# Six SBUF homes instead of seven for the experts' gate/up weights, with the residual x left in place

## The reference

```python
x = x + mixer(rmsnorm(x, norm_mix[i]))
h = rmsnorm(x, norm_ffn[i])
# router: best group of 4, then the best 2 of its 8 experts, with their gates -> combine
hid = silu(einsum('td,edf->tef', h, w_gate)) * einsum('td,edf->tef', h, w_up)
x = x + einsum('tef,efd->td', hid * combine[..., None], w_down)
```

## Time and profile before

| | |
|---|---|
| median of 3 runs | 1291.3 us (1290.79 to 1293.12) |
| the profiled execution, own time | 1287.51 us |
| its span | 1285.7 us |
| PE busy | 1138.3 us (89%) |
| DVE, ACT, POOL busy | 530.9, 379.7, 388.3 us |
| DMA | 278.21 MB, mean 216 GB/s |
| chain that ended last | PE 63%, DMA 14%, DVE 10%, SP's queue 7%, ACT 4% |

### The profile page before, as it was taken

One profiled execution on the slowest core, in us unless ns is written; L12 is line 12 of the kernel. 1 busy time (PEld: TensorE's weight loads), 2 busy tenths in 40 slices (PEclk: granted clock), 3 DMA queues, 4 the chain that ended last, 5 costly groups with the idle time before them and its releaser, 6 DMA issues.

```text
span 1285.7 us, 21203 instructions
## 1 busy us (share of the span) xinstructions
PE 1138.3 (89%) x8573; PEld 796.6 (62%) x8573; DVE 530.9 (41%) x1202; ACT 379.7 (30%) x838; POOL 388.3 (30%) x428
## 2 busy tenths in 40 slices
PE   5999999799999883989779999779999899999792
PEld 4866678555555442868568887568888555555341
DVE  4466763411111115565685455764653411111114
ACT  3426841111111012364453445443522011111010
POOL 1334521122322211057545366442301022322210
PEclk9999999899999896989899999899999799999997
DMA  7121047999999998011000130001458899999996
GB/s 239 66 73 67 2 197 282 379 375 384 380 383 381 384 396 316 11 66 66 1 3 2 66 117 15 2 3 65 165 182 328 345 365 383 386 384 379 379 392 248
DMA packets 67793, 278.21 MB, mean 216 GB/s; under 512 B 16888, under 2 KB 16984, under 8 KB 43120
## 3 DMA queue, kind: packets, MB, share of 16 engines
q1 hardware_dynamic: 56480, 255.89, 52.4%
q0 software_dynamic: 11072, 20.43, 4.7%
q10 hardware_dynamic: 144, 0.52, 0.1%
HBM read 265.83 MB, written 27.26 MB: 228 GB/s over the span
## 4 chain that ended last, share of the span: by engine, by line
PE 63%; DMA 14%; DVE 10%; SPq 7%; ACT 4%; issue 2%; POOL 1%; DVEq 0%; POOLq 0%
PE bank L1101 11%; PE bank L150 9%; PE bank L152 9%; PE bank L151 9%; DMA hn<-in_moe_w_up 5%; PE bank L1110 5%; SPq L2332 4%; PE bank L1643 4%; PE bank L1093 3%; DMA ring<-in_moe_w_up 3%; DMA arena<-in_moe_w_up 2%; SPq L2338 2%; DMA ring<-in_gdn_w_in 2%; PE bank L519 2%; PE bank L528 1%
## 5 line engine op out<-in xcount | busy, mean ns | idle before, releaser
L978 POOL DMA_INDIRECT y_rows<-arena,idx_i x64 | 64.6, 1010 | 348.5 <-DVE arena L1287 343.5
L1192 ACT ACTIVATE arena<-bank 128x128 f32<-128x128 f32 x64 | 17.8, 277 | 367.2 <-PE bank L1101 202.0
L1291 DVE TENSOR_TENSOR arena<-arena,bank 128x128 f32<-128x128 f32 x64 | 18.4, 288 | 258.3 <-ACT arena L1192 258.3
L152 PE MATMUL bank<-ring_r,ht_r 128*128 128x512 f32 x288 | 113.1, 393 | 0.0
L1101 PE MATMUL bank<-ring,arena 128*64 128x256 f32 x832 | 101.6, 395 | 8.9 <-DMA ring<-in_moe_w_up 7.9
L1287 DVE COPY arena<-bank 128x512 f32<-128x512 f32 x64 | 44.3, 692 | 143.9 <-PE bank L1110 143.9
L150 PE MATMUL bank<-ring_r,arena_r 128*128 128x512 f32 (+1 forms) x228 | 91.5, 401 | 4.8 <-DVE ring_r L174 4.8
L151 PE MATMUL bank<-ring_r,arena_r 128*128 128x512 f32 x224 | 88.0, 393 | 0.0
L1101 PEld LDWEIGHTS bank<-ring,arena 128*64 128x64 f32 x832 | 57.6, 136 | 44.1 <-DMA ring<-in_moe_w_up 8.9
L151 PE MATMUL bank<-ht_r,ring_r 128*128 128x512 f32 (+1 forms) x224 | 81.8, 365 | 0.0
L1093 PEld LDWEIGHTS bank<-ident,arena 64*128 64x128 f32 x512 | 61.3, 201 | 28.4 <-issue 25.1
(11 more groups left out here) (339 smaller groups left out, 2342.9 us busy)
## 6 DMA issues: line engine op xcount, KB each, us to landing
ring<-in_moe_w_gate SPq DMA_DIRECT2D x26, 1024.0 KB
ring<-in_moe_w_up SPq DMA_DIRECT2D x26, 1024.0 KB
arena<-in_moe_w_down SPq DMA_DIRECT2D x24, 1024.0 KB
ring<-in_moe_w_down SPq DMA_DIRECT2D x24, 1024.0 KB
ring<-in_gdn_w_in SPq DMA_DIRECT2D x8, 2048.0 KB, 8.3
arena<-in_moe_w_gate SPq DMA_DIRECT2D x10, 1024.0 KB
arena<-in_moe_w_up SPq DMA_DIRECT2D x10, 1024.0 KB
ht<-in_moe_w_gate SPq DMA_DIRECT2D x10, 1024.0 KB
```

The source lines that it names most:

```text
L152: return pe.matmul(dst, a[1], b[0], start=False, stop=stop)
L978: pool.indirect_dma_start(out=y_rows[l], out_offset=bass.IndirectOffsetOnAxis(ap=idx_i[:, 1, e:e + 1], axis=0), in_=y_out[:, e % RING, :], ...
```

## The change

Home 6 is gone, with the store of x, the read-back, and the waits on both. Expert e uses gate/up home e mod 6 up to e = 30, and expert 31 uses home 3. The homes of the down matrices and the waits on all other homes are as before. The order of SP's queue is otherwise unchanged.

```diff
-        x_rows = [dram(f"x_rows{l}", [SEQ, D]) for l in range(2)]
...
-        GU_SLOTS, DN_SLOTS = 7, 8
+        GU_SLOTS, DN_SLOTS = 6, 8
...
-                   ht[:, :, :].rearrange("p c n -> p (c n)"), hn[:, :, :].rearrange("p t n -> p (t n)"),
-                   x[:, :, :].rearrange("p t n -> p (t n)")]
-        X_HOME, GAIN2_HOME = 6, 7
+                   ht[:, :, :].rearrange("p c n -> p (c n)"), hn[:, :, :].rearrange("p t n -> p (t n)")]
+        GAIN2_HOME = 7
...
-        GU_OF = [e % GU_SLOTS for e in range(EXPERTS - 4)] + [0, 3, 4, 5]
+        GU_OF = [e % GU_SLOTS for e in range(EXPERTS - 1)] + [3]
...
-        x_kept, x_again = sem("x_kept"), sem("x_again")
...
         def combine_best(dve, t, o):
-            if t == 0:
-                dve.wait_ge(x_again, 16 * TT)
...
         def finish_dve(dve, o):
-            dve.wait_ge(x_again, 16 * TT * 2)
...
-            x_spilled = [(x_kept, 16 * TT * (l + 1)), (ln["rows"], TT * (2 * l + 2))]
-            gu_freed = [None, half_way, half_way, done, [(s["routed"], TT * (l + 1))], kept_rows, x_spilled]
+            gu_freed = [None, half_way, half_way, done, [(s["routed"], TT * (l + 1))], kept_rows]
...
-            for t in range(TT):
-                sp.wait_ge(x_half, 2 * TT * l + TT + t + 1)
-                sp.dma_start(x_rows[l][t * P:(t + 1) * P, :], x[:, t, :]).then_inc(x_kept, 16)
             load_gate_up(sp, l, 3, gu_freed[3])
             for k in (4, 5, 6):
                 load_down(sp, l, k, dn_freed[k])
-            for e in (4, X_HOME, 5):
+            for e in (4, 5):
                 load_gate_up(sp, l, e, gu_freed[e])
             for e in range(GU_SLOTS, EXPERTS):
                 load_gate_up(sp, l, e, None)
...
-            sp.wait_ge(s["up"], EXPERTS * l + max(e for e in range(EXPERTS) if GU_OF[e] == X_HOME) + 1)
-            for t in range(TT):
-                sp.dma_start(x[:, t, :], x_rows[l][t * P:(t + 1) * P, :]).then_inc(x_again, 16)
```

## The result

The changed kernel takes 1297.87 us in the median of ten runs, against 1291.43 for the kernel before: ratio 1.0053, 95% interval 1.0038 to 1.0069, so 5 to 9 us slower. The forecast was 1300.6 us (9.3 us slower) with a range of 1295 to 1308. The profiled execution of the changed kernel took 1295.35 us, its span is 1293.4 us, 7.7 us more than before.

The account below looks back on a forecast made before the run. The prediction took the arrival of the last gate/up pair to bound each expert loop. Plus 3.1 us at layer 0's combine and 6.2 us in layer 1's loop made 9.3 us, from 1291.3 to 1300.6 us, range 1295 to 1308.

Parts of the forecast that it names:

- What bounds: Both expert loops: the arrival of the last gate/up pair, expert 31's, sets the end, at 482.3 and 1254.6 us.
- Store: Ahead of each loop: dropping the 2 MiB store of x is worth 0, at best 0 to 1 us.
- One pair moves: Start of each loop: 77 MiB instead of 75 pass between hn's pair and expert 31's, 5.4 us more (4.9 to 6.2).
- Expert 31 waits for gate/up of 27: End of each loop: expert 31's home frees later, but over 20 us of transfers are still queued, so 0.
- One down matrix slips: Start of each loop: down 8 queues behind pair 8, the second step issues 2 MiB instead of 3, costing 0.8 us.
- Read-back in layer 1: Behind the second loop: the read-back was hidden by PE's last expert and the scatter, so dropping it is worth 0.
- Combine in layer 0: Behind the first loop: scatter lands in 2.4 us, first combine at 506.0 instead of 502.87, held by y: plus 3.1 us.
- Expert 0 unmoved: Start of the loops: expert 0 begins at the same time as in the kernel before.
- SP's issuing: Rival: SP's issuing, not transport, sets the arrival; loops end as before, panel issued sooner, minus 3 us, 1288.3; 6%.
- no difference: Rival: idle gaps at the loops' start absorb the extra pair, costing 3.9 and 2.4 us; 1293.5 us in all; 9%.
- Slower by much more: Rival: 3.12 us per MiB, the whole slipped matrix and a 5.4 us scatter, 17.7 us more, 1309; 20%.

Follow-up runs that it names:

- six_store: Changed kernel with the store of x put back but no read-back: 1300.45 us, ratio 1.0071.
- six_store_readback: Changed kernel with the store of x and its read-back both at their old places, so only the home is taken away: 1299.60 us, ratio 1.0058.
- six_down8_early: Changed kernel with down matrix 8 alone issued one step earlier, behind pair 7 instead of pair 8: 1299.11 us, ratio 1.0053.
- six_mid_read: Changed kernel with x stored as before and read back in the middle of each loop, behind expert 16's weights: 1317.61 us, ratio 1.0202.
- five_homes: Changed kernel with hn's home gone too, leaving five gate/up homes: 1314.68 us, ratio 1.0152.
- six_down_early: Changed kernel with all queued down matrices issued one step earlier, putting down 31 ahead of expert 31's pair: 1305.45 us, ratio 1.0093.
- six_down_late: Changed kernel with each down matrix issued one step later, behind the next expert's pair: 1295.13 us, ratio 1.0028.
- six_again: Changed kernel repeated with nothing edited, beside the kernel before on the same chip: 1299.28 us, ratio 1.0053.
- seven_x_split: Kernel before, layer 0's panel issued first, then x blocks 0 and 1, with blocks 2 and 3 between the reads of y: 1288.89 us, ratio 0.9984.
- seven_panel_first: Kernel before with layer 0's read-back of x issued behind the GDN panel instead of ahead of it: 1290.43 us, ratio 0.9976.
- seven_down_late: Kernel before with each down matrix issued one step later, behind the next expert's pair: 1289.97 us, ratio 0.9977.
- seven_down_late_x_split: Kernel before with down matrices one step later and the read-back of x in two halves: 1286.05 us, ratio 0.9961.

## Why the prediction was right, and where it was off

*What bounds.* Right: expert 31 waits for its up-weights in both loops, before and after, and the read in the middle shows that more bytes make the loop longer wherever they stand.

*Store.* Predicted 0 to 1 us per layer; six_store shows none in the loops and the start, and its median leaves room for a microsecond or two elsewhere.

*One pair moves.* Predicted 5.4 us per loop. Measured, as the mean of four profiles with six homes against three with seven: 235.0 - 229.7 = 5.3 and 237.0 - 231.4 = 5.6. The DMA engines' idle time ahead of hn's pair was 9 us in layer 0 rather than 5, since the queue was already empty at 242 (share 0.11 in 242 to 244 us) and hn's pair came 1.6 us later. PE's waits for weights grew by 4.6 us in the first loop and by 4.9 in the second (13.1 to 18.0), not quite the 6 that were forecast.

*Expert 31 waits for gate/up of 27.* Predicted 0. SP does wait there, from 454.0 to 457.98 us, but the DMA share is 1.01 to 1.03 in each 10 us from 440 to 480, so the wait is covered, as the prediction had it.

*One down matrix slips.* Predicted 0.8 us per loop, measured about 0. This is the term that was mis-sized, together 1.6 us of the sum. The step that issues only 2 MiB is filled by them and the gathers all the same (DMA share 0.97 in 264.3 to 271.2 us of the changed kernel), and the one behind it has 0.91, which is 0.6 us of idle engines. That is less than the loops differ between two profiles of the same kernel.

*Read-back in layer 1.* Predicted 0. The rest of the second loop is 30.5 us against 31.1; six_store_readback has 31.3. It may have been worth half a microsecond, but six_down8_early, without a read-back, has 31.1 as well, so this is within the noise.

*Combine in layer 0.* Predicted a tail of 17.5 us (506.0 - 488.5) with y as the late one, measured 17.8, with the scatter at 2.72 us (I had taken 2.4) and DVE waiting for y. Right, and the store-and-read-back run confirms the cause.

*Expert 0 unmoved.* Wrong in the pair of profiles, where it is 1.6 us later. The windows say how: from 222.5 us to hn's pair PE's granted clock was 0.77 instead of 0.88. In all 14 profiles the start lies between 253.2 and 257.4. The four that start at 253.2, two with seven homes and two with six, have a clock of 0.89 from 222 us to expert 0, the other ten 0.79 to 0.84. So the start goes with the clock and not with the number of homes; what decides the clock is not shown.

*The rivals.* "SP's issuing" (6%) and "no difference" (9%) had their chance from small doubts. The first falls with six_mid_read. The second falls with the loops, 5.3 and 5.6 us longer where it wanted 3.9 and 2.4: the gaps at the start of the loops did not take in the extra pair and are still there, shares of 0.83 and 0.88 in layer 0 and 0.81 and 0.81 in layer 1 of the changed kernel. "Slower by much more" needed 3.12 us per MiB and the slipped matrix in full; neither occurred.

*The size.* The stages that the change moves give 5.3 + 5.6 - 2.8 - 0.5 = 7.6 us. The measured 6.4 us (4.9 to 8.9) and the repeat's ratio agree with it. The forecast was 9.3, and 1.6 of the excess is the slip. In the pair of profiles the difference of 7.7 us comes out near this sum partly by luck: the later start (+1.6) and the shorter middle (-1.1), which the change does not touch, nearly cancel.

**Still open: the middle.** It takes 519 to 522 us in eleven profiles and 528 to 530 in three (six_mid_read, five_homes, six_down_early), though the code there is the same. Two stretches at about the same distance behind the combine, 120 and 300 us in the kernel before (first two lines), 118 and 300 us in six_mid_read (last two):

```profile
622.90:682.90 60.00, 44.36 (x988) 33.97 (x989) 45.66 (x103) 28.72 (x78) 29.06 (x40) 0.94 0.01 2
...
802.90:862.90 60.00, 45.01 (x1005) 35.71 (x1004) 43.16 (x100) 28.79 (x76) 28.94 (x38) 0.94 0.01 2
```

```profile
628.90:688.90 60.00, 46.84 (x945) 35.43 (x945) 45.43 (x99) 27.96 (x79) 29.19 (x38) 0.89 0.01 2
...
810.60:870.60 60.00, 47.29 (x964) 35.88 (x962) 45.99 (x100) 27.69 (x79) 29.40 (x38) 0.89 0.01 3
```

The granted clock is 0.89 instead of 0.94, and fewer matmuls fit in. The combine comes late in all three (508.9 to 514.5 us), but in six_down_late (509.5) and six_store_readback (510.1) it comes as late, and their middle is short. The times of all executions say a little more. The five of six_mid_read took 1314.89 to 1321.69 us at a mean clock of 0.946 to 0.951, and the fastest of them is the one profiled, with its long middle. So for this kernel it hardly is a chance of single executions. Of five_homes two took 1308.06 and 1308.5 us at 0.956, the other four 1313.48 to 1318.43 at 0.946 to 0.953, so there it may be. No run here tells what decides it, so these 8 us of six_mid_read, five_homes and six_down_early are counted neither for nor against a theory.

## What to carry to other kernels

Where a queue of weights is full to the end, as here with five, six and seven homes, more room in it does not help; what matters is how many bytes have to pass between the last moment it was empty and the last operand. A buffer that is filled ahead of that moment is worth its bytes, here 5.3 and 5.6 us for 2 MiB, and storing and fetching 2 MiB to free it was cheap here, 2.8 us in one tail and nothing that stood out of the noise elsewhere. Before giving up such a buffer, look at the order of the queue: issuing each down matrix one step later gained 2 us in the medians with seven homes and 3 to 4 with six. Moving bytes away from a small write whose landing is on the path shortened one tail by 2.7 us, but not in the second kernel that tried it, so that is worth a trial and no more.

## What the runs showed that I had not expected

The landing time of a scatter of a few rows goes with the loads beside it. The last one of layer 0 landed in 2.7 to 2.9 us where the DMA share in the microsecond before its issue was 0.04 to 0.23 (the changed kernel, six_again, six_down_late, seven_x_split), and in 5.4 to 5.7 us where it was 0.71 to 0.85 (the kernel before, six_store_readback, seven_panel_first, seven_down_late, seven_down_late_x_split). The last of these had only half of x ahead, so what counts is what is still underway and not the size of the read-back; why the loads hold the scatter up is not shown.

A wait of PE for weights can cost more than its length. After waits of 2.61 and 3.71 us the 32 matmuls took 5.33 and 6.61 us instead of 3.85, at a granted clock of 0.70 and 0.50; after one of 2.58 us they took 3.84, at 1.00. While the transport sets the end this is hidden; with the down matrices issued later it was what limited the first loop.

The same kernel's time moves by several us from run to run (1289.73 to 1298.0 for the kernel before), and between profiles the clock ahead of the loop and in the middle differs. Differences of 1 to 3 us were readable only stage by stage.
